# Four weight slots with the low part written in place, four bank pairs in the input loops: a two-layer diffusion trunk on one Trainium2 core

## The chip, the cores and the metric

The kernel runs on one core of a Trainium2 chip. The metric is the device time of one execution in microseconds (us), the median of several runs. A core has these engines: TensorE (PE in the profile) for matrix products, VectorE (DVE), ScalarE (ACT), GpSimd (POOL), and SyncE (SP), whose in-order queue issues nearly all DMA transfers here. Engines run side by side and order themselves by semaphores: an instruction waits until a semaphore has reached a number.

## The reference, cut to what matters

384 tokens (128 context, 256 latent) of width 1024 go through two layers. Each layer is a half-step FFN, a mixer, and a second half-step FFN; so there are four FFNs, which hold most of the arithmetic:

```python
def swiglu(h, w_in, w_out):                       # w_in 1024 x 5632, w_out 2816 x 1024
    gate, up = jnp.split(h @ w_in, 2, axis=-1)
    return (jax.nn.silu(gate) * up) @ w_out

def macaron_layer(x, mod, norm_g, ffn_in, ffn_out, mixer):
    m = mod[:, :, None, :]                        # mod = silu(cond) @ w_mod + b_mod
    x = x + 0.5 * m[:, 2] * swiglu(modulate(x, norm_g[0], m[:, 0], m[:, 1]), ffn_in[0], ffn_out[0])
    mixed, own_kv = mixer(modulate(x, norm_g[1], m[:, 3], m[:, 4]))
    x = x + m[:, 5] * mixed
    x = x + 0.5 * m[:, 8] * swiglu(modulate(x, norm_g[2], m[:, 6], m[:, 7]), ffn_in[1], ffn_out[1])
    return x, own_kv
```

Layer 0 mixes by attention beside a convolution, layer 1 by a Fourier mix beside a gated unit. Inputs are fp32, and `mod` is a product of two conditioning vectors with a 1024 x 9216 matrix in each layer.

## The kernel before

**Units.** All projection weights are cut into 153 units of 128 x 2048 fp32 values (1 MB) that are used in one fixed order: 33 for an FFN, 11 and 10 for the mixers. In an FFN the units 0 to 21 are input units (a gate tile and an up tile each) and 22 to 32 are output units. The text counts units from the start of an FFN. The code calls the four FFNs s = 0, 2, 3, 5; the text says first to fourth.

**The path of a unit.** SP loads it into a slot of `w_raw`; ACT copies it, rounded, to `w_hi` (`split` on ACT); DVE writes `w_lo = w_raw - w_hi` (`split` on DVE); PE runs 48 matmuls on it (`three`: hi*hi, hi*lo, lo*hi for each of 16 blocks). There are RING = 3 slots of each of the three tensors. The load of unit u waits until `w_lo` of unit u-3 is written (`lo_done`), since then the raw values are dead; ACT's `split` of u waits until PE is through with u-3 (`unit_done`), since then `w_hi` is free.

**Input loop.** `step` t of ACT and DVE first splits unit t+2; then ACT takes silu of the gate of unit t, DVE multiplies it by the up part, and both split the result into `h_hi` and `h_lo`. PE's unit t writes bank pair t % 3 of the PSUM, so it waits for the product of unit t-3 (`prod_done`).

**Output units** accumulate into all eight PSUM banks. The first one takes them in an order that starts with the banks that the last input units have left first.

**Modulation tiles.** `mod` for later stages is made on DVE beside the FFNs: a tile is a 128 x 1024 piece of `w_mod` (0.5 MB), multiplied by each of two conditioning rows with a sum along the row (`mod_tile`, two instructions). Three tile slots lie in the first halves of `m_raw`; the other halves hold the two rows and a scratch row for the first product. SP's load of tile n waits for tile n-3 (`tile_used`).

**Order on the queues.** SP, ACT and DVE execute in the order in which the code is written. SP's `load_ffn` and DVE's `ffn` mix units and tiles by hand-written tables: `TILES_BEFORE` tiles ahead of the loop, one tile in each loop step, then `TILES_OUT[s][j]` tiles in output iteration j, in which DVE splits unit 24+j and SP loads a unit and then that many tiles.

**End of an FFN.** Behind its last tiles DVE makes the gate, adds the eight 128-row blocks of the output to `x` (`residual`, which waits block by block for PE), and ACT and POOL sum the squares for the next norm. PE can only start the next stage when that norm is through.

Of the kernel before, what the change touches and what calls it, by code (L numbers as in the profile page):

```python
# [21 lines left out]
F32R = mybir.dt.float32r  # L22
# [4 lines left out]
P = 128  # L27
# [26 lines left out]
RING = 3  # L54
MRING = 3
UNIT = 2048
# [15 lines left out]
LOOPS = (FT - 1) // RING  # L72
FIRST_TILES = MRING * GROUPS_FIRST * PAIR_TILES
MOD_TILES = 2 * MODT - FIRST_TILES
TILES_BEFORE = {0: 3, 2: 0, 3: 0, 5: 2}
TILE_LOOPS = {0: LOOPS, 2: LOOPS, 3: LOOPS, 5: 2}
TILES_OUT = {0: [3, 3] + [2] * 8, 2: [2] + [1] * 9, 3: [3] + [2] * 8 + [0], 5: [0] * 10}
TILE0, _t = {}, 0
for _s in (0, 2, 3, 5):
    TILE0[_s] = _t  # L80
    _t += TILES_BEFORE[_s] + MRING * TILE_LOOPS[_s] + sum(TILES_OUT[_s])
assert _t == MOD_TILES and MRING == RING
# [87 lines left out]
def build(nc, x_prompt, x_sample, cache_k, cache_v, c, c_ctx, b_mod, norm_g,  # L170
# [4 lines left out]
    with ctx:  # L175
# [94 lines left out]
        tile_in = [sem(f"tile_in{i}") for i in range(MRING)]  # L270
# [61 lines left out]
        def mod_rows(b):  # L332
            return m_raw[:, b, 0:D_MODEL]

        def cond_row(cnd):
            return m_raw[:, cnd, D_MODEL:UNIT]

        def row_products():
            return m_raw[:, 2, D_MODEL:UNIT]
# [3 lines left out]
        def _(sp):  # L343
            def load_unit(u, i=0):

                sp.wait_ge(lo_done, u + 1 + RING * i)
                sp.dma_start(w_raw[:, slot(u), :].unsqueeze(1),
                             w_units[bass.ds(u + i * RING, 1)].rearrange("u p n -> p u n")).then_inc(raw_in[slot(u)], 16)
# [8 lines left out]
            def load_tile(n, i=0):  # L357

                if n >= MRING:
                    sp.wait_ge(tile_used, n - MRING + 1 + MRING * i)  # L360
                sp.dma_start(mod_rows(n % MRING).unsqueeze(1),
                             w_rows[bass.ds(n + MRING * i, 1)].rearrange("t p n -> p t n")).then_inc(tile_in[n % MRING], 16)

            def load_ffn(s):
# [137 lines left out]
        def _(act):  # L502
# [46 lines left out]
            def ffn(s):  # L549
# [12 lines left out]
                step(0, 0, 0)  # L562
                with act.Fori(0, LOOPS) as i:
                    for b in range(RING):
                        step(1 + b, (1 + b) % RING, i)
# [212 lines left out]
        def _(dve):  # L778
# [27 lines left out]
            def mod_tile(n, i=0):  # L806

                dve.wait_ge(tile_in[n % MRING], 16 * (n // MRING + 1) + 16 * i)
                if n:
                    dve.wait_ge(half_used, n + MRING * i)  # L810
                for cnd, out, done in ((0, row_products(), half_used), (1, mod_rows(n % MRING), tile_used)):
                    nc.vector.scalar_tensor_tensor(  # L812
                        out, mod_rows(n % MRING), 1.0, cond_row(cnd), ALU.mult, ALU.mult,
                        accum_out=mod_cols[:, bass.ds(FIRST_TILES + n + MRING * i, 1), cnd]).then_inc(done, 1)
# [73 lines left out]
            def ffn(s):  # L888
# [20 lines left out]
                step(0, 0, 0, None)  # L909
                done = 0  # L910
                for rounds, with_tiles in ((TILE_LOOPS[s], True), (LOOPS - TILE_LOOPS[s], False)):
                    if rounds:
                        with dve.Fori(0, rounds) as i:
                            for b in range(RING):
                                step(1 + RING * done + b, (1 + b) % RING, i, n + b if with_tiles else None)
                        done += rounds
                n += MRING * TILE_LOOPS[s]
# [262 lines left out]
        def _(pe):  # L1180
# [92 lines left out]
            def ffn(s):  # L1273
# [8 lines left out]
                with pe.Fori(0, LOOPS - 1) as i:  # L1282
                    for b in range(RING):
                        step(2 + b, i)
                for t in range(2 + RING * (LOOPS - 1), FT):
                    step(t, 0)
# [17 lines left out]
                with pe.Fori(0, (FFN_OUT_UNITS - 2) // RING) as i:  # L1304
                    for b in range(RING):
                        out_unit(u0 + FT + 1 + b, 1 + b, i)
                u = u0 + FFN_UNITS - 1
# [314 lines left out]
```

## Time and profile before

| what | value |
|---|---|
| median of 3 runs | 1500.81 us (1499.41 to 1501.71) |
| profiled execution | 1499.5 us, span in the profile 1497.7 us |
| PE busy | 1407.8 us, 94% of the span |
| DVE busy | 970.0 us, 65% |
| ACT busy | 557.7 us, 37% |
| DMA | 242.96 MB, mean 162 GB/s |

The profile is of one execution. Times of rows are in us from its start; "busy" counts an engine's own instructions, and a row's bracket says how long the engine was idle before it and what ended that. PE's share says that it is nearly always at work, so what counts is where it is not, and what would make it wait in new places.

### The profile page before, as it was taken

To read this page: it belongs to the slowest core of one execution; us is meant where nothing else is said; L and a number is where in the kernel's file an instruction comes from. 1 tells how busy PE (TensorE), PEld (TensorE's weight loads), DVE (VectorE), ACT (ScalarE), POOL (GpSimd) and SP (SyncE) were. 2 spreads that over 40 slices of the span, in tenths; PEclk is the share of its full clock that TensorE was granted. 3 is DMA by queue.
4 is the path that set the end of the run, shared out by engine and by line. 5 is a ranking of instruction groups with operands and counts; after the bars stand their busy time and mean duration, and the time that the engine had idled before them with its cause. 6 is when DMAs were issued, how large, how long until landed. Compare 5 with 4: busy or idle time off the path is not lost.

```text
span 1497.7 us, 21193 instructions
## 1 busy us (share of the span) xinstructions
PE 1407.8 (94%) x8134; PEld 1375.4 (92%) x8134; DVE 970.0 (65%) x1394; ACT 557.7 (37%) x731; POOL 122.5 (8%) x110
## 2 busy tenths in 40 slices
PE   5799999989866899999998999999989989999998
PEld 3799999989845799999998999999989989999998
DVE  2777678968998566666757666679763477444332
ACT  2433332237666443333224333332345343333221
POOL 1000000014555100000001000000021010000000
PEclk9899999989878999999998999999989999999999
DMA  8765655752200235555652555547523325433421
GB/s 325 261 231 176 203 177 200 285 182 96 86 32 29 102 133 201 188 191 174 234 181 85 197 193 185 193 149 295 219 99 134 126 85 186 137 122 130 141 84 42
DMA packets 45114, 242.96 MB, mean 162 GB/s; under 512 B 4997, under 2 KB 6889, under 8 KB 24328
## 3 DMA queue, kind: packets, MB, share of 16 engines
q1 hardware_dynamic: 44464, 241.99, 46.7%
q8 instruction: 32, 0.52, 0.1%
q10 hardware_dynamic: 600, 0.30, 0.1%
q14 instruction: 18, 0.15, 0.0%
HBM read 240.57 MB, written 1.70 MB: 162 GB/s over the span
## 4 chain that ended last, share of the span: by engine, by line
PE 83%; DVE 10%; DMA 2%; ACT 2%; issue 1%; POOL 1%; ACTq 0%; SPq 0%; DVEq 0%; POOLq 0%
PE ps L1185 27%; PE ps L1186 27%; PE ps L1187 27%; DVE conv L974 4%; DVE w_lo L790 1%; DMA conv_rows<-in_conv_w 1%; DVE n_full L876 1%; PE ps L1254 1%; DVE m_raw L812 1%; DVE smax L1039 1%; ACT w_hi L528 1%; DVE a_lo L883 0%; POOL n_acc L453 0%; DMA m_raw<-in_w_pairs 0%; PE ps L1554 0%
## 5 line engine op out<-in xcount | busy, mean ns | idle before, releaser
L1185 PE MATMUL ps<-a_hi,w_hi 128*128 128x384 f32 x1744 | 591.7, 339 | 19.1 <-DVE a_lo L883 14.0
L1186 PE MATMUL ps<-a_lo,w_hi 128*128 128x384 f32 x1744 | 588.5, 337 | 0.0
L1187 PE MATMUL ps<-a_hi,w_lo 128*128 128x384 f32 x1744 | 588.1, 337 | 0.0
L790 DVE TENSOR_TENSOR w_lo<-w_raw,w_hi 128x2048 fp32r<-128x2048 f32 x153 | 352.9, 2306 | 162.3 <-ACT w_hi L528 162.0
L528 ACT ACTIVATE w_hi<-w_raw 128x2048 fp32r<-128x2048 f32 x153 | 292.1, 1909 | 264.7 <-PE ps L1187 200.2
L1185 PEld LDWEIGHTS ps<-a_hi,w_hi 128*128 128x128 f32 x1744 | 332.1, 190 | 23.4 <-issue 10.0
L1186 PEld LDWEIGHTS ps<-a_lo,w_hi 128*128 128x128 f32 x1744 | 332.1, 190 | 0.1
L1187 PEld LDWEIGHTS ps<-a_hi,w_lo 128*128 128x128 f32 x1744 | 331.7, 190 | 0.0
L812 DVE SCALAR_TENSOR_TENSOR m_raw<-m_raw 128x1024 f32<-128x1024 f32 x252 | 296.0, 1220 | 1.0 <-ACT m_raw L589 1.0
L1187 PE MATMUL ps<-h_hi,w_lo 128*128 (+1 forms) x704 | 236.6, 336 | 0.0
L1186 PE MATMUL ps<-h_lo,w_hi 128*128 (+1 forms) x704 | 236.6, 336 | 0.0
L1185 PE MATMUL ps<-h_hi,w_hi 128*128 (+1 forms) x704 | 236.6, 336 | 0.0
L557 ACT ACTIVATE glu<-ps 128x384 f32<-128x384 f32 x88 | 43.4, 493 | 376.6 <-PE ps L1187 376.6
L895 DVE TENSOR_TENSOR glu<-glu,ps 128x384 f32<-128x384 f32 x88 | 48.7, 554 | 167.2 <-ACT glu L557 167.2
L1187 PEld LDWEIGHTS ps<-h_hi,w_lo 128*128 128x128 f32 x704 | 132.4, 188 | 0.0
L1185 PEld LDWEIGHTS ps<-h_hi,w_hi 128*128 128x128 f32 x704 | 132.4, 188 | 0.0
L1186 PEld LDWEIGHTS ps<-h_lo,w_hi 128*128 128x128 f32 x704 | 132.4, 188 | 0.0
L898 DVE TENSOR_TENSOR h_lo<-glu,h_hi 128x384 f32 (+1 forms) x88 | 49.2, 559 | 71.6 <-ACT h_hi L559 71.6
L453 POOL TENSOR_TENSOR n_acc<-n_sq 128x384 f32<-128x384 f32 x6 | 6.1, 1014 | 973.4 <-ACT n_sq L538 879.5
L559 ACT ACTIVATE h_hi<-glu 128x384 f32 (+1 forms) x88 | 46.2, 525 | 86.4 <-DVE glu L895 86.4
L473 POOL TENSOR_TENSOR conv<-conv,taps_buf 128x399 f32<-128x399 f32 x60 | 72.9, 1215 | 51.5 <-ACT taps_buf L618 45.6
L974 DVE SCALAR_TENSOR_TENSOR conv<-padded,conv_wt,conv 128x399 f32<-128x399 f32 x60 | 61.1, 1018 | 1.6
(179 smaller groups left out, 666.2 us busy)
## 6 DMA issues: line engine op xcount, KB each, us to landing
w_raw<-in_w_units SPq DMA_DIRECT2D x153, 1024.0 KB, 5.0
m_raw<-in_w_rows SPq DMA_DIRECT2D x126, 512.0 KB, 3.6
m_raw<-in_w_pairs SPq DMA_DIRECT2D x9, 1024.0 KB, 7.7
out<-x_nat SPq DMA_DIRECT2D x3, 512.0 KB, 3.1
x_nat<-in_x_sample SPq DMA_DIRECT2D x1, 1024.0 KB, 12.5
fourier<-in_k_fourier SPq DMA_DIRECT2D x1, 768.0 KB, 4.4
x_nat<-in_x_prompt SPq DMA_DIRECT2D x1, 512.0 KB, 10.7
m_raw<-in_c_ctx SPq DMA_DIRECT2D x1, 512.0 KB, 5.7
```

The source lines that it names most:

```text
L473: nc.gpsimd.tensor_tensor(acc, acc, taps_buf[:, n % TAP_BUFS, :], ALU.add).then_inc(tap_added, 1)
L528: nc.scalar.activation(w_hi[:, slot(u), :], w_raw[:, slot(u), :], ACT.Copy).then_inc(hi_done, 1)
L557: nc.scalar.activation(glu[:, 0, :], ps[:, 2 * b, 0:TOK], ACT.Silu).then_inc(silu_done, 1)
L559: nc.scalar.activation(h_hi[:, bass.ds(t + RING * i, 1), :], glu[:], ACT.Copy).then_inc(h_hi_done, 1)
L790: nc.vector.tensor_tensor(w_lo[:, slot(u), :], w_raw[:, slot(u), :], w_hi[:, slot(u), :].bitcast(FP32), ALU.subtract).then_inc(lo_done, 1)
L812: nc.vector.scalar_tensor_tensor(out, mod_rows(n % MRING), 1.0, cond_row(cnd), ALU.mult, ALU.mult, accum_out=mod_cols[:, bass.ds(FIRST_TIL ...
L895: nc.vector.tensor_tensor(glu[:, 0, :], glu[:, 0, :], ps[:, 2 * b + 1, 0:TOK], ALU.mult).then_inc(prod_done, 1)
L898: nc.vector.tensor_tensor(h_lo[:, bass.ds(t + RING * i, 1), :], glu[:], h_hi[:, bass.ds(t + RING * i, 1), :].bitcast(FP32), ALU.subtract). ...
L974: ins = nc.vector.scalar_tensor_tensor(conv[:, j, :], padded[:, j, k:k + CONV_N], conv_wt[:, j, k:k + 1], conv[:, j, :], ALU.mult, ALU.add)
L1185: mm(out, whi, mhi, start=start, stop=False)
L1186: mm(out, whi, mlo, start=False, stop=False)
L1187: return mm(out, wlo, mhi, start=False, stop=stop)
```

## The change

Both rings get a fourth place. `RING` becomes 4; `w_lo` shares its memory with `w_raw`, so that DVE writes the low part over the raw values. A raw slot is then free only when PE is through with the unit, and SP's load of unit u waits for `unit_done` of u-4. The tile ring becomes 4 (`TRING`): four tile slots fill `m_raw` slots 0 and 1, the two conditioning rows fill slot 2, and the scratch row is a new tensor `m_prod`. PE's input unit t uses bank pair t % 4. The loops have five rounds of four steps instead of seven of three, and the tables are written anew; each FFN keeps its number of tiles (46, 32, 40, 8).

```diff
-RING = 3
+RING = 4
 MRING = 3
+TRING = 4
@@
-LOOPS = (FT - 1) // RING
+LOOPS = (FT - 2) // RING
@@
-TILES_BEFORE = {0: 3, 2: 0, 3: 0, 5: 2}
+TILES_BEFORE = {0: TRING, 2: 0, 3: 0, 5: 0}
 TILE_LOOPS = {0: LOOPS, 2: LOOPS, 3: LOOPS, 5: 2}
-TILES_OUT = {0: [3, 3] + [2] * 8, 2: [2] + [1] * 9, 3: [3] + [2] * 8 + [0], 5: [0] * 10}
+TILES_OUT = {0: [3] * 2 + [2] * 8, 2: [2, 2] + [1] * 8, 3: [2] * 10, 5: [0] * 10}
@@
-        w_raw = sb("w_raw", [P, RING, UNIT])
+        r = ExitStack()
+        w_raw = sb("w_raw", [P, RING, UNIT], stack=r)
+        r.close()
+        w_lo = sb("w_lo", [P, RING, UNIT], F32R)
         w_hi = sb("w_hi", [P, RING, UNIT], F32R)
-        w_lo = sb("w_lo", [P, RING, UNIT], F32R)
         m_raw = sb("m_raw", [P, MRING, UNIT])
+        m_prod = sb("m_prod", [P, D_MODEL])
@@
             def load_unit(u, i=0):
 
-                sp.wait_ge(lo_done, u + 1 + RING * i)
+                sp.wait_ge(unit_done, u + 1 + RING * i)
@@
             def load_tile(n, i=0):
 
-                if n >= MRING:
-                    sp.wait_ge(tile_used, n - MRING + 1 + MRING * i)
+                if n >= TRING:
+                    sp.wait_ge(tile_used, n - TRING + 1 + TRING * i)
@@
-                n += MRING * TILE_LOOPS[s]
+                n += TRING * TILE_LOOPS[s]
                 for j, tiles in enumerate(TILES_OUT[s]):
-                    if j < FFN_OUT_UNITS - 2:
-                        load_unit(u0 + FT + 2 + j)
+                    load_unit(u0 + FT + 1 + j)
                     for _ in range(tiles):
                         load_tile(n)
                         n += 1
@@
                 step(0, 0, 0, None)
+                step(1, 1, 0, None)
@@
-                        for d in (2, 3, 4, 5, 6, 7, 0, 1) if first else range(KT):
-                            if first and h == 0 and d in (2, 4, 0):
-                                pe.wait_ge(prod_done, RING + FT * f + FT - {2: 2, 4: 1, 0: 0}[d])
+                        for d in (4, 5, 6, 7, 0, 1, 2, 3) if first else range(KT):
+                            if first and h == 0 and d % 2 == 0:
+                                pe.wait_ge(prod_done, RING + FT * f + FT - {4: 3, 6: 2, 0: 1, 2: 0}[d])
```

**DVE at the start of the first FFN.** The rows are DVE's instructions from the subtraction for unit 1 to the first step; two rows that read `m_raw` are one tile, and L790 is the subtraction for unit 2. Before:

```order
L790 TENSOR_TENSOR w_lo<-w_raw,w_hi 128x2048 [waits hi_done]
L812 SCALAR_TENSOR_TENSOR m_raw,mod_cols<-m_raw 128x1024 [waits tile_in0,silu_rows]
L812 SCALAR_TENSOR_TENSOR m_raw,mod_cols<-m_raw 128x1024
...
L812 SCALAR_TENSOR_TENSOR m_raw,mod_cols<-m_raw 128x1024 [waits half_used,tile_in2]
L812 SCALAR_TENSOR_TENSOR m_raw,mod_cols<-m_raw 128x1024
L790 TENSOR_TENSOR w_lo<-w_raw,w_hi 128x2048 [waits hi_done]
L895 TENSOR_TENSOR glu<-glu,ps 128x384 [waits silu_done]
```

And now:

```order
L791 TENSOR_TENSOR w_lo<-w_raw,w_hi 128x2048 [waits hi_done]
L813 SCALAR_TENSOR_TENSOR m_prod,mod_cols<-m_raw 128x1024 [waits tile_in0,silu_rows]
L813 SCALAR_TENSOR_TENSOR m_raw,mod_cols<-m_raw 128x1024
...
L813 SCALAR_TENSOR_TENSOR m_prod,mod_cols<-m_raw 128x1024 [waits half_used,tile_in3]
L813 SCALAR_TENSOR_TENSOR m_raw,mod_cols<-m_raw 128x1024
L791 TENSOR_TENSOR w_lo<-w_raw,w_hi 128x2048 [waits hi_done]
L896 TENSOR_TENSOR glu<-glu,ps 128x384 [waits silu_done]
```

Four tiles instead of three stand ahead of the subtraction for unit 2.

**SP behind the input loop of the first FFN.** `m_raw<-in_w_rows` is a tile's load, `w_raw<-in_w_units` a unit's. Before, the first row loads unit 24, and each unit stands ahead of the tiles of its own iteration:

```order
L347 DMA w_raw<-in_w_units 128x2048 [waits lo_done]
L361 DMA m_raw<-in_w_rows 128x1024 [waits tile_used] x3
L347 DMA w_raw<-in_w_units 128x2048 [waits lo_done]
L361 DMA m_raw<-in_w_rows 128x1024 [waits tile_used] x3
L347 DMA w_raw<-in_w_units 128x2048 [waits lo_done]
L361 DMA m_raw<-in_w_rows 128x1024 [waits tile_used] x2
```

Now the rows have the same form, but the first one loads unit 23:

```order
L348 DMA w_raw<-in_w_units 128x2048 [waits unit_done]
L362 DMA m_raw<-in_w_rows 128x1024 [waits tile_used] x3
L348 DMA w_raw<-in_w_units 128x2048 [waits unit_done]
L362 DMA m_raw<-in_w_rows 128x1024 [waits tile_used] x3
L348 DMA w_raw<-in_w_units 128x2048 [waits unit_done]
L362 DMA m_raw<-in_w_rows 128x1024 [waits tile_used] x2
```

So unit 24, which was loaded ahead of the tiles of iteration 0, now stands behind them, and unit 24+j behind those of iteration j; a tile's load waits for the tile four before it, not three, and a unit's for PE instead of DVE.

## Rows read from the trace of the kernel before

**Rows 1.** The page, part 1: busy time, share of the span, instructions.

```profile
PE 1407.8 (94%) x8134; PEld 1375.4 (92%) x8134; DVE 970.0 (65%) x1394; ACT 557.7 (37%) x731; POOL 122.5 (8%) x110
```

**Rows 2.** Waits of PE: in total, how often, the longest (us).

```profile
PE ps L1185 <- DVE a_lo L883: 14.0, 6, 2.9
...
PE ps L1185 <- DVE w_lo L790: 3.3, 2, 1.7
```

**Rows 3.** Timeline of PE: the first matmuls of units 2, 3 and 26.

```profile
67.53 0.45 PE L1185 MATMUL ps<-a_hi,w_hi 128*128 128x384 f32 x1 [1.60 <-DVE w_lo L790]
...
75.97 0.33 PE L1185 MATMUL ps<-a_hi,w_hi 128*128 128x384 f32 x1
...
267.32 0.34 PE L1185 MATMUL ps<-h_hi,w_hi 128*128 x1
```

**Rows 4.** Timeline of DVE: third tile, then the subtraction for unit 2.

```profile
62.90 1.22 DVE L812 SCALAR_TENSOR_TENSOR m_raw<-m_raw 128x1024 f32<-128x1024 f32 x1
...
64.05 1.22 DVE L812 SCALAR_TENSOR_TENSOR m_raw<-m_raw 128x1024 f32<-128x1024 f32 x1
...
65.19 2.29 DVE L790 TENSOR_TENSOR w_lo<-w_raw,w_hi 128x2048 fp32r<-128x2048 f32 x1
```

**Rows 5.** Timeline of SP's queue behind the input loop of the first FFN.

```profile
239.00 0.33 SPq L361 DMA_DIRECT2D m_raw<-in_w_rows  x1
239.37 0.43 SPq L347 DMA_DIRECT2D w_raw<-in_w_units  x1
243.49 4.91 SPq L361 DMA_DIRECT2D m_raw<-in_w_rows  x3
248.45 0.43 SPq L347 DMA_DIRECT2D w_raw<-in_w_units  x1
...
255.79 0.43 SPq L347 DMA_DIRECT2D w_raw<-in_w_units  x1
```

**Rows 6.** Timeline of ACT there: the copies for units 25 and 26.

```profile
246.56 1.92 ACT L528 ACTIVATE w_hi<-w_raw 128x2048 fp32r<-128x2048 f32 x1 [8.78 <-DMA w_raw<-in_w_units]
255.97 1.92 ACT L528 ACTIVATE w_hi<-w_raw 128x2048 fp32r<-128x2048 f32 x1 [7.49 <-DMA w_raw<-in_w_units]
```

**Rows 7.** Timeline of DVE there: subtractions for units 22, 23, 24.

```profile
222.36 2.29 DVE L790 TENSOR_TENSOR w_lo<-w_raw,w_hi 128x2048 fp32r<-128x2048 f32 x1
...
230.65 2.29 DVE L790 TENSOR_TENSOR w_lo<-w_raw,w_hi 128x2048 fp32r<-128x2048 f32 x1
...
238.89 2.29 DVE L790 TENSOR_TENSOR w_lo<-w_raw,w_hi 128x2048 fp32r<-128x2048 f32 x1
```

**Rows 8.** DMA issues of 90 to 220, 236 to 264, 1020 to 1056 us: median landing.

```profile
w_raw<-in_w_units SPq DMA_DIRECT2D x16, 1024.0 KB, 5.1
...
w_raw<-in_w_units SPq DMA_DIRECT2D x4, 1024.0 KB, 7.5
...
w_raw<-in_w_units SPq DMA_DIRECT2D x5, 1024.0 KB, 5.8
```

**Rows 9.** Loads of units from 200 to 330 us, all.

```profile
DMA to landing us min/median/max: 4.9/6.2/9.8
```

**Rows 10.** Timelines around the end of the first FFN: DVE, PE.

```profile
315.57 2.29 DVE L790 TENSOR_TENSOR w_lo<-w_raw,w_hi 128x2048 fp32r<-128x2048 f32 x1 [5.95 <-ACT w_hi L528]
...
322.78 5.29 DVE L852 SCALAR_TENSOR_TENSOR x<-ps,m_gate,x 128x128 f32<-128x128 f32 x16
...
325.39 0.34 PE L1187 MATMUL ps<-h_hi,w_lo 128*128 128x384 f32 x1
...
339.03 0.69 PE L1185 MATMUL ps<-a_hi,w_hi 128*128 128x384 f32 x1 [2.14 <-DVE a_lo L883]
```

**Rows 11.** The same places at the end of the third FFN.

```profile
1081.20 0.74 DVE L852 SCALAR_TENSOR_TENSOR x<-ps,m_gate,x 128x128 f32<-128x128 f32 x2 [4.91 <-PE ps L1187]
...
1088.03 0.34 PE L1187 MATMUL ps<-h_hi,w_lo 128*128 128x384 f32 x1
...
1097.72 0.66 PE L1185 MATMUL ps<-a_hi,w_hi 128*128 128x384 f32 x1 [2.23 <-DVE a_lo L883]
```

More of the change, by code:

```diff
@@ L80 @@
     TILE0[_s] = _t
-    _t += TILES_BEFORE[_s] + MRING * TILE_LOOPS[_s] + sum(TILES_OUT[_s])
-assert _t == MOD_TILES and MRING == RING
+    _t += TILES_BEFORE[_s] + TRING * TILE_LOOPS[_s] + sum(TILES_OUT[_s])
+assert _t == MOD_TILES and TRING == RING
 LAYER_PAIRS = MODT // PAIR_TILES
@@ L269, in build @@
         mod_used = sem("mod_used")
-        tile_in = [sem(f"tile_in{i}") for i in range(MRING)]
+        tile_in = [sem(f"tile_in{i}") for i in range(TRING)]
         half_used, tile_used = sem("half_used"), sem("tile_used")
@@ L332, in mod_rows @@
         def mod_rows(b):
-            return m_raw[:, b, 0:D_MODEL]
+            return m_raw[:, b // 2, b % 2 * D_MODEL:(b % 2 + 1) * D_MODEL]
         def cond_row(cnd):
-            return m_raw[:, cnd, D_MODEL:UNIT]
-        def row_products():
-            return m_raw[:, 2, D_MODEL:UNIT]
+            return mod_rows(TRING + cnd)
         @block.sync
@@ L562, in ffn @@
                 step(0, 0, 0)
+                step(1, 1, 0)
                 with act.Fori(0, LOOPS) as i:
                     for b in range(RING):
-                        step(1 + b, (1 + b) % RING, i)
+                        step(2 + b, (2 + b) % RING, i)
                 split(u0 + FT + 2)
@@ L806, in mod_tile @@
             def mod_tile(n, i=0):
-                dve.wait_ge(tile_in[n % MRING], 16 * (n // MRING + 1) + 16 * i)
+                dve.wait_ge(tile_in[n % TRING], 16 * (n // TRING + 1) + 16 * i)
                 if n:
-                    dve.wait_ge(half_used, n + MRING * i)
-                for cnd, out, done in ((0, row_products(), half_used), (1, mod_rows(n % MRING), tile_used)):
+                    dve.wait_ge(half_used, n + TRING * i)
+                for cnd, out, done in ((0, m_prod[:], half_used), (1, mod_rows(n % TRING), tile_used)):
                     nc.vector.scalar_tensor_tensor(
-                        out, mod_rows(n % MRING), 1.0, cond_row(cnd), ALU.mult, ALU.mult,
-                        accum_out=mod_cols[:, bass.ds(FIRST_TILES + n + MRING * i, 1), cnd]).then_inc(done, 1)
+                        out, mod_rows(n % TRING), 1.0, cond_row(cnd), ALU.mult, ALU.mult,
+                        accum_out=mod_cols[:, bass.ds(FIRST_TILES + n + TRING * i, 1), cnd]).then_inc(done, 1)
             def mod_ready(tiles):
@@ L914, in ffn @@
                             for b in range(RING):
-                                step(1 + RING * done + b, (1 + b) % RING, i, n + b if with_tiles else None)
+                                step(2 + RING * done + b, (2 + b) % RING, i, n + b if with_tiles else None)
                         done += rounds
-                n += MRING * TILE_LOOPS[s]
+                n += TRING * TILE_LOOPS[s]
                 for j, tiles in enumerate(TILES_OUT[s]):
@@ L1281, in ffn @@
                 first_units(u0, (0, 2), s, s != 0)
-                with pe.Fori(0, LOOPS - 1) as i:
+                with pe.Fori(0, LOOPS) as i:
                     for b in range(RING):
                         step(2 + b, i)
-                for t in range(2 + RING * (LOOPS - 1), FT):
-                    step(t, 0)
                 def out_unit(u, t, i, first=False):
@@ L1303, in ffn @@
                 pe.wait_ge(h_ready, 1 + FT * (f + 1))
-                with pe.Fori(0, (FFN_OUT_UNITS - 2) // RING) as i:
+                rounds = (FFN_OUT_UNITS - 2) // RING
+                with pe.Fori(0, rounds) as i:
                     for b in range(RING):
                         out_unit(u0 + FT + 1 + b, 1 + b, i)
+                for t in range(1 + RING * rounds, FFN_OUT_UNITS - 1):
+                    out_unit(u0 + FT + t, t, 0)
                 u = u0 + FFN_UNITS - 1
```

4 lines of the change are left out of this document (2 added, 2 removed).

## The prediction, made before the changed kernel was run

> **What bounds the kernel now.** I read the page's busy times first: PE works 94% of the span [rows 1]. Then PE's waits. The only ones inside an FFN's run of units are two for `w_lo`, 3.3 us together [rows 2]; the rest sits where a norm or a mixer stands between two runs. The timeline of PE shows the second of the two: unit 2 starts at 67.53 after a wait, unit 3 at 75.97, unit 26 at 267.32 [rows 3]. That is 191.35 us for 23 units, 8.32 us each, so from unit 3 on PE never paused. This says at once what the fourth bank pair can bring: a product that PE waits for doesn't occur in PE's list, so it removes nothing. The same holds for a deeper ring in the steady part. A gain can only lie where PE stands still now, and a loss wherever the new order makes a unit late by more than its lead.
>
> **Start of the first FFN.** DVE runs the tiles ahead of the subtraction for unit 2, and PE waits for exactly that subtraction: it starts at 65.19, directly behind the third tile, and PE starts at 67.53, directly behind it [rows 3, 4]. A tile takes 65.19 - 62.90 = 2.29 us [rows 4]. The fourth tile stands in the same place, with nothing to cover it: **+2.3 us**. DVE's backlog is not passed on further: everything behind moves by the same 2.3 us, PE too. The tile that is saved in step 1 comes after the subtraction that matters. In what follows I use the times of the old trace, without these 2.3 us.
>
> **Input loops.** A unit's load now waits until PE is through with the unit four before. ACT wants unit t+2 only behind the work for unit t-1; the load starts when unit t-2 ends, one unit (8.32 us) earlier, and such loads land in 5.1 us [rows 8]. So some 3 us and the silu work for unit t-1 cover it, and behind that PE's own lead of a unit; if that cover went, ACT would be late by the difference, and PE would see it only beyond some 5 us more. The mixers I cost at nothing for the same reason: their loads are issued when the fourth unit before ends, and ACT's copy stands behind the second or third.
>
> **Output units of the first FFN.** Here the order on SP's queue decides. Iteration j held: load unit 24+j, then its tiles. Now unit 24+j stands behind the tiles of iteration j, and a tile's load waits for the tile four before, which DVE must have finished. So a unit's load waits for DVE, and DVE's next subtraction waits for that load: a loop through four parts. I work it out by these pieces:
>
> - from the end of a tile on DVE to the issue of the unit's load behind it: the tile's own issue first, then 0.37 us [rows 5], together 0.45 us;
> - landing L;
> - ACT's copy 1.92 us, DVE's subtraction 2.2 us, with the handovers 4.25 us. The old rows agree: issued at 248.45, copy begun at 255.97 [rows 5, 6].
>
> For L there are rows of both kinds: four loads around 250 us landed in 7.5 (median), five at 1020 to 1056 us in 5.8 [rows 8]; in both places each followed a tile's load closely. I take 7.1 for unit 25 and 7.4 for unit 26, which go out where the old loads were slow, and 5.8 after them.
>
> Now in order. The tile of step 20 ends at 230.65, where the subtraction for unit 23 starts [rows 7]; unit 24's load goes at 231.1 and is there before DVE wants it at 238.9 [rows 7]. The three tiles of iteration 0 end at 243.5, 245.8, 248.1. The third tile of iteration 1 waits for the second of these, and unit 25 behind it is issued at 246.2; it went at 239.37 [rows 5]. Its low part is ready at 246.2 + 7.1 + 4.25 = 257.6; PE wants it at 267.32 - 8.32 = 259.0. Then comes the first tile of iteration 1, until 259.9, which releases unit 26's load at 260.3 (it went at 248.45 [rows 5]). Ready at 260.3 + 7.4 + 4.25 = 272.0, wanted at 267.3: **PE stands for 4.7 us**.
>
> From there every second unit closes the loop: two tiles (4.6), 0.45, L, 4.25, in sum 15.1 us at L = 5.8, against 16.64 us that PE takes for two units. So PE waits no more, but DVE gains only 1.5 us on PE in two units. Low parts of units 28, 30, 32 are ready at 287.1, 302.2, 317.3; the two tiles behind the last, the subtraction for unit 33 (2.2), two more tiles (4.6) and the gate (0.4) put the residual at 329.1. It started at 322.78 [rows 10]. PE, 4.7 us later than before, is through with its last unit at about 330, so the residual, 5.3 us long, is behind PE there too, and the norm behind it moves with it: **+6.3 us**. The stall of PE is inside this sum and isn't added to it.
>
> The old boundary was late already: from the last matmul to the first of the next stage 13.6 us (325.39, 339.03), where the third FFN needs 9.7 (1088.03, 1097.72) since its DVE waited 4.9 us for PE before the residual [rows 10, 11]. That 3.9 us is all that this place could give back.
>
> **The other FFNs.** The second has one tile in most iterations, so DVE's share of the loop halves and the loads are soon released by PE alone: nothing. The third now has two tiles in every iteration, the last one included. By the same recurrence, with L = 5.8 to 6.5, its gate is ready before PE delivers the first block: nothing; at 7.4 it is 4 us late. The fourth has no tiles in its output part.
>
> **Sum.** 2.3 + 6.3 = 8.6 us. The profiled execution took 1499.5 us, 1.3 below the median; on the median this gives 1500.8 + 8.6 = **1509.4 us**. A measurement tells 0.2% (3 us) from no change.
>
> **What L does.** L = 5.75 throughout gives the residual at 325.9 (+3.1, sum 5.4, 1506.2 us). L = 7.4 throughout gives a loop of 16.7 us, as long as PE's, the residual at 334.2 (+11.4), and with the third FFN's 4 us a sum of 17.7: 1518.5 us. The page "DMA: Bandwidth & Descriptors" of the Trainium skill, in its section on the anatomy of one DMA, prices a transfer at about 2.0 us plus its bytes over 436 GB/s (it fits another issuing path); by it a unit alone would take an estimated 4.4 us and a unit with the tile ahead of it 5.6. With 4.4 the sum would be near -1.5 us, with 5.6 near +4.6. The old trace doesn't agree with the lower of these: its fastest load in this stretch took 4.9, the median was 6.2 [rows 9].
>
> **Rivals.**
>
> *The loop keeps up (not slower).* One mechanism: loads land fast enough that unit 26 isn't late and DVE catches up. With L = 4.8 unit 26 is ready at 267.0, the loop takes 14.1 us, and the residual comes at 321.2, 1.6 us earlier than now. With the start's 2.3 us that is 1501.5 us. It turns into a gain only below L = 4.7. For it: single loads of 4.9 us [rows 9], and less traffic from one side, since loads are spaced further apart. Against it: every one of these loads has a tile's load right ahead of it, and such ones took 5.8 or more in the median [rows 8]. The Trainium skill ("Trainium Kernel Development and Optimization", Best Practices) advises double buffering so that DMA and compute overlap; read simply, a fourth place should help. Its gain would have to come from the 3.9 us above.
>
> *Every load is slow.* L near 7.4 throughout and the third FFN late too: 1514 to 1518.5 us. For it: the four loads around 250 us [rows 8]. Against: those overlapped the unit before, which the new spacing avoids.
>
> *Only the start costs.* If I have the queue's waits wrong and units are still ahead, the sum is 2.3 us: 1503 us. Against it stand the rows of SP above: the tiles' loads came out at DVE's pace even with the old order [rows 5].
>
> *The mixers.* If a raw load there came late, ACT would hold back the taps for POOL, 1 to 3 us. PE's list has no wait for `w_lo` there that it would lengthen [rows 2]; I leave it in the range.
>
> **How the numbers follow.** Forecast (5 to 12 us slower, PE late at unit 26 and a late residual): 0.60. Loop slow throughout or the third FFN late as well, above 1513: 0.16. Only the start or a loop that nearly keeps up, 1500 to 1504: 0.16. A gain of over 3 us, for which landing would have to be under 4.7 and the start hidden: 0.05; a loss from a place that I cost at nothing (the mixers, an input loop): 0.03. Range: 1502 to 1517 us; the forecast's own is 1505 to 1513. Slower by over 0.2%: 0.79, within 0.2%: 0.16, faster: 0.05.
>
> **What would show it.** PE's wait for `w_lo` before unit 2 grows from 1.6 to 3.9 us. A new wait of PE for `w_lo`, 2 to 6 us, stands before unit 26, the fifth output unit of the first FFN. SP issues unit 25 some 7 us later against PE than now and unit 26 some 12. DVE's subtractions there wait for ACT, and ACT for `w_raw`'s DMA, every second unit. From the last matmul of the first FFN to the next stage it is 13.6 us plus 1 to 3 instead of 9.7. The three other FFNs keep units of 8.32 us and their boundaries. I am wrong if unit 26 isn't late, if the boundary falls to 10 us, or if waits turn up in the input loops or the mixers.

## The result and the profile after

| | before | after |
|---|---|---|
| median of 5 runs each, side by side | 1501.71 us (1499.41 to 1503.12) | 1514.75 us (1512.49 to 1519.90) |
| profiled execution, span | 1499.5, 1497.7 us | 1515.96, 1514.2 us |
| mean granted clock | 0.964 | 0.959 |

The changed kernel is slower: the ratio is 1.0091, 95% interval 1.0076 to 1.0107. On the medians that is 13.0 us, between the two profiled executions 16.5 us. This difference and all but one of those below are under 2%; where an interval leaves out 1, I call the kernel slower or faster.

Busy times of the page, then PE's waits for `w_lo`, as in [rows 1, 2]:

```profile
PE 1417.0 (94%) x8134; PEld 1383.7 (91%) x8134; DVE 969.4 (64%) x1394; ACT 559.3 (37%) x731; POOL 120.2 (8%) x110
```

```profile
PE ps L1187 <- DVE w_lo L791: 9.4, 4, 3.9
```

The work is the same, and yet PE is busy 9.2 us longer. Waits for `w_lo` are 9.4 us instead of 3.3. The first number can't be a wait: the same 8134 matmuls took longer. 2.7 us of it are in unit 2, as shown next, and 5.1 us in the first mixer (see "Left open" below). The timeline of PE shows the places, as in [rows 3, 10]: units 2, 3, 26, then the last matmul of the first FFN and the first of the mixer.

```profile
69.23 0.69 PE L1187 MATMUL ps<-a_hi,w_hi 128*128 128x384 f32 x1 [3.86 <-DVE w_lo L791]
...
74.84 0.52 PE L1189 MATMUL ps<-a_hi,w_lo 128*128 128x384 f32 x1
...
75.38 0.33 PE L1188 MATMUL ps<-a_lo,w_hi 128*128 128x384 f32 x1
...
80.41 0.33 PE L1187 MATMUL ps<-a_hi,w_hi 128*128 128x384 f32 x1
...
275.01 0.44 PE L1187 MATMUL ps<-h_hi,w_hi 128*128 x1 [3.08 <-DVE w_lo L791]
...
334.22 0.34 PE L1189 MATMUL ps<-h_hi,w_lo 128*128 128x384 f32 x1
...
352.71 0.69 PE L1187 MATMUL ps<-a_hi,w_hi 128*128 128x384 f32 x1 [2.14 <-DVE a_lo L884]
```

Unit 2 waits 3.86 us instead of 1.60, and then its matmuls stand 0.32 us apart until 75 us, and 0.17 us after that. It takes 11.18 us, not 8.44. The windows say the same of the clock (columns: window, its length, busy us of PE, PEld, DVE, ACT and POOL with their instructions, granted clock, DMA share, GB/s). After:

```profile
70.00:80.00 10.00, 10.00 (x45) 10.00 (x45) 6.16 (x5) 4.71 (x5) 0.00 (x0) 0.74 0.11 43
```

And before:

```profile
70.00:80.00 10.00, 10.00 (x60) 10.00 (x59) 8.28 (x9) 3.94 (x6) 0.00 (x0) 1.00 0.80 285
```

PE is busy in all ten microseconds of both, but has 45 matmuls there where it had 60; the mean granted clock is 0.74, so it was at the lower level (1.2 of 2.4 GHz) for about the first half.

Output units of the first FFN: SP's queue [rows 5], ACT's copies for units 25 and 26 [rows 6], and DVE's subtractions for them:

```profile
250.60 0.43 SPq L348 DMA_DIRECT2D w_raw<-in_w_units  x1
252.52 12.27 SPq L362 DMA_DIRECT2D m_raw<-in_w_rows  x2
264.83 0.43 SPq L348 DMA_DIRECT2D w_raw<-in_w_units  x1
```

```profile
257.90 1.92 ACT L528 ACTIVATE w_hi<-w_raw 128x2048 fp32r<-128x2048 f32 x1 [14.84 <-DMA w_raw<-in_w_units]
270.62 1.91 ACT L528 ACTIVATE w_hi<-w_raw 128x2048 fp32r<-128x2048 f32 x1 [10.80 <-DMA w_raw<-in_w_units]
```

```profile
259.84 2.29 DVE L791 TENSOR_TENSOR w_lo<-w_raw,w_hi 128x2048 fp32r<-128x2048 f32 x1 [7.35 <-ACT w_hi L528]
...
272.56 2.29 DVE L791 TENSOR_TENSOR w_lo<-w_raw,w_hi 128x2048 fp32r<-128x2048 f32 x1 [3.56 <-ACT w_hi L528]
...
329.29 2.29 DVE L791 TENSOR_TENSOR w_lo<-w_raw,w_hi 128x2048 fp32r<-128x2048 f32 x1 [1.68 <-ACT w_hi L528]
...
336.49 5.29 DVE L853 SCALAR_TENSOR_TENSOR x<-ps,m_gate,x 128x128 f32<-128x128 f32 x16
```

Every link of the loop is there: the queue stands 12 us at a tile's load, the unit's load goes when DVE has ended a tile, ACT waits for that load, DVE for ACT, PE for DVE. Since unit 3 began 4.44 us later than before, a time of the old trace is one of these less 4.44. The residual comes at 332.05 by the old clock instead of 322.78 [rows 10], and it never waits for PE.

From here "start to start of unit u" is the time from the first matmul of unit u-1 to that of unit u, over the whole program (33 is the mixer's first unit, 44, 77 and 110 are the first of the next three stages, 120 that of the last FFN). In us, from the timelines of PE; the names are those of the experiments below:

| unit | before | after | e1 | e2 | e3 | e4 | e6 | e12 | e8 | e10 |
|---|---|---|---|---|---|---|---|---|---|---|
| 2 | 10.19 | 12.48 | 10.20 | 12.49 | 10.20 | 10.20 | 10.19 | 10.20 | 10.19 | 10.20 |
| 3 | 8.44 | 11.18 | 8.43 | 11.11 | 8.45 | 8.46 | 8.43 | 8.43 | 8.44 | 8.44 |
| 26 | 8.32 | 11.57 | 10.98 | 8.32 | 8.33 | 8.32 | 8.32 | 8.32 | 8.32 | 8.32 |
| 27 | 8.32 | 8.42 | 10.00 | 8.32 | 8.32 | 8.32 | 8.32 | 8.32 | 8.32 | 8.32 |
| 28 | 8.32 | 9.27 | 8.32 | 8.32 | 8.32 | 8.32 | 8.32 | 8.32 | 8.32 | 8.32 |
| 33 | 21.79 | 26.64 | 24.95 | 16.93 | 16.93 | 17.74 | 26.83 | 25.71 | 16.92 | 16.92 |
| 44 | 17.70 | 17.02 | 17.01 | 17.02 | 17.01 | 17.70 | 23.66 | 19.06 | 17.01 | 16.92 |
| 77 | 17.83 | 17.02 | 17.01 | 17.02 | 17.02 | 17.84 | 24.02 | 19.06 | 16.91 | 17.01 |
| 110 | 17.84 | 17.88 | 21.03 | 17.03 | 16.85 | 17.69 | 23.72 | 19.06 | 17.02 | 17.02 |
| 120 | 17.01 | 16.97 | 16.80 | 17.02 | 17.02 | 17.02 | 22.16 | 19.06 | 17.01 | 16.83 |

The first FFN accounts for 2.29 (wait before unit 2) + 2.74 (its low clock) + 3.25 + 0.10 + 0.95 (units 26 to 28) + 4.85 (boundary) = 14.2 us of the loss between the two profiled executions. The first mixer adds 3.4 us, the boundaries at 44 and 77 give 1.5 back.

### The profile page after: what moved, and what is told of

Same layout as the page of the kernel before. It is cut to its first block, busy times and chain, and to the rows that moved or that the text cites. A ratio compares the mean times of both kernels' runs of the same rounds, so it can differ in the third digit from the quotient of the medians.

```text
span 1514.2 us, 21053 instructions
## 1 busy us (share of the span) xinstructions
PE 1417.0 (94%) x8134; PEld 1383.7 (91%) x8134; DVE 969.4 (64%) x1394; ACT 559.3 (37%) x731; POOL 120.2 (8%) x110
## 4 chain that ended last, share of the span: by engine, by line
PE 78%; DVE 12%; DMA 4%; ACT 2%; issue 2%; POOL 1%; ACTq 0%; SPq 0%; DVEq 0%; POOLq 0%
PE ps L1187 25%; PE ps L1188 25%; PE ps L1189 25%; DVE conv L976 4%; DMA w_raw<-in_w_units 2%; DVE w_lo L791 2%; DVE m_prod L813 1%; DMA conv_rows<-in_conv_w 1%; ACT w_hi L528 1%; DVE n_full L877 1%; PE ps L1256 1%; DVE m_raw L813 1%; DVE smax L1041 1%; DVE a_lo L884 0%; POOL n_acc L453 0%
## 5 line engine op out<-in xcount | busy, mean ns | idle before, releaser
L813 DVE SCALAR_TENSOR_TENSOR m_prod<-m_raw 128x1024 f32<-128x1024 f32 x126 | 153.6, 1219 | 1.0 <-ACT m_raw L590 1.0
L813 DVE SCALAR_TENSOR_TENSOR m_raw<-m_raw 128x1024 f32<-128x1024 f32 x126 | 153.8, 1220 | 0.0
```

Source lines behind the costliest of these rows:

```text
L813: nc.vector.scalar_tensor_tensor(out, mod_rows(n % TRING), 1.0, cond_row(cnd), ALU.mult, ALU.mult, accum_out=mod_cols[:, bass.ds(FIRST_TIL ...
```

## The experiments

Each ran in five rounds beside the kernel before, whose medians in the three sets were 1502.36, 1502.40 and 1501.96 us.

**The fourth tile behind step 1** (e1), on DVE alone:

```diff
-                for _ in range(TILES_BEFORE[s]):
+                late = 1 if s == 0 else 0
+                for _ in range(TILES_BEFORE[s] - late):
                     mod_tile(n)
                     n += 1
                 step(0, 0, 0, None)
                 step(1, 1, 0, None)
+                for _ in range(late):
+                    mod_tile(n)
+                    n += 1
```

> The changed kernel, with DVE's fourth tile of the first FFN moved from ahead of step 0 to behind step 1; nothing else. Theory (the start costs a tile plus the low clock that the longer wait brings): unit 2 of PE waits 1.6 us as in the kernel before instead of 3.9 and runs at 8.4 us instead of 11.2; 2.3 + 2.7 = 5 us less than the changed kernel, about 1510 us against 1502 of before; the output part of the first FFN keeps its loss of about 9 us. Rival (the slow unit 2 has another cause, such as DMA traffic of the earlier loads beside it): unit 2 stays at 11 us, and only 2.3 us come back.

Measured 1509.72 us (1508.13 to 1513.20), ratio 1.0053 (1.0039 to 1.0068): 5.0 us under the changed kernel. Units 2 and 3 are back at 10.20 and 8.43 us. One tile of 2.3 us cost 5.0, as the wait that it made longer cost the clock too (e7 below shows that). The output part of the first FFN lost 7.5 us here (units 26, 27 and 33 of the table), not 9. The profiled execution of e1, the slowest of its six, was late by 3.2 us at unit 110, the end of the third FFN, where DVE's residual ran through without a wait for PE, which had been 4.91 us [rows 11]:

```profile
1094.62 5.29 DVE L853 SCALAR_TENSOR_TENSOR x<-ps,m_gate,x 128x128 f32<-128x128 f32 x16
```

**A unit's load ahead of its tiles again** (e2), SP alone:

```diff
-                    load_unit(u0 + FT + 1 + j)
+                    if j == 0:
+                        load_unit(u0 + FT + 1)
+                    if j < FFN_OUT_UNITS - 2:
+                        load_unit(u0 + FT + 2 + j)
```

> The changed kernel, with SP's order behind the input loops as before: unit 24+j ahead of the tiles of iteration j (unit 33 still behind them). Theory (the loss of the output part is the loop SP - DMA - ACT - DVE that this order closed): the waits of PE before units 26 and 28 vanish, the subtractions for units 25 to 33 no longer wait for late loads, the residual of the first FFN waits for PE, and the way from the last matmul to the next stage falls from 16.2 us to the 9.7 of the third FFN: 13 us less than the changed kernel, about 1502 us, level with before. Rival (the tile ring of four or the loads' wait for PE is the cause, not the place in the queue): the stall at unit 26 stays and the time falls by under 3 us.

Measured 1499.93 us (1497.63 to 1502.04), ratio 0.9985 (0.9976 to 0.9993). That is 14.8 us under the changed kernel, where 13 were expected. Units 26 to 28 are at 8.32 us and the boundary at 16.93, which is 4.9 better than before, though the order is that of before. The timelines of DVE and of SP show where that comes from:

```profile
318.87 0.17 DVE L848 TENSOR_TENSOR m_gate<-mod_cols,vec_a 128x16 f32<-128x16 f32 x1
...
323.07 0.74 DVE L856 SCALAR_TENSOR_TENSOR x<-ps,m_gate,x 128x128 f32<-128x128 f32 x2 [3.82 <-PE ps L1192]
```

```profile
297.35 5.39 SPq L362 DMA_DIRECT2D m_raw<-in_w_rows  x4
305.30 25.29 SPq L348 DMA_DIRECT2D w_raw<-in_w_units  x4
```

DVE now waits 3.8 us for PE ahead of the residual, which it had started at once [rows 10]. The first of the four loads of units is issued at 305.30, 300.8 by the old clock (unit 3 began 4.5 us later than before here), against 307.73 in the kernel before. I read it so that with four tile slots the last tiles' loads wait for earlier tiles and the queue gets past them sooner; that alone wasn't tried.

**Both repairs, and the load of unit 33 ahead of the last tiles** (e3): e1's and e2's edits and the lines below, which hold for the first three FFNs. The load is taken out of its old place at the start of the next stage (not shown).

```diff
-                    if j < FFN_OUT_UNITS - 2:
+                    if j < FFN_OUT_UNITS - 2 or s < 5:
```

> Both repairs together: fourth tile behind step 1, units ahead of the tiles, and unit 33 too ahead of the last tiles. Theory: nothing of the loss stays, and the first FFN's boundary is down to 9.7 us, so 3.5 to 4 us less than the kernel before: about 1498 us. Rival (the four slots or the write in place cost something by themselves, such as in the mixers): at or above 1502 us.

Measured 1494.86 us (1493.77 to 1497.04), ratio 0.9956 (0.9943 to 0.9969): faster than both kernels, and 3 us under the 1498 expected.

**That load alone, in the kernel before** (e4):

> The kernel before (three slots), with only the load of unit 33 moved ahead of the last iteration's tiles. Theory (the late boundary of the first FFN came from this load): it goes at 305 us instead of 307.7, the residual starts about 2.7 us earlier, and the time falls by 2 to 3 us to 1499: most of what the four slots bring after repair would be had without them. Rival (a deeper ring is needed for it): no change, 1502 us.

Measured 1498.68 us (1495.84 to 1499.69), ratio 0.9975 (0.9967 to 0.9984). The edit moves the same load in the first three FFNs, but only the boundary at 33 changes much: it falls by 4.1 us, those at 77 and 110 by 0.2 at most. So the 3.9 us read from [rows 10, 11] were there to be had. Between e4 and e3 lie 3.8 us that neither theory had: the table shows 0.7 to 0.8 us at each of units 33, 44, 77 and 110. The timelines around unit 77, of POOL, DVE and ACT, first of the kernel before:

```profile
799.02 4.47 POOL L453 TENSOR_TENSOR n_acc<-n_acc,n_sq 128x384 f32<-128x384 f32 x4
```

```profile
802.45 0.17 DVE L835 TENSOR_TENSOR m_shift<-mod_cols,vec_b 128x16 f32<-128x16 f32 x1
802.53 0.99 DVE L836 TENSOR_TENSOR m_scale<-mod_cols,vec_b 128x16 f32<-128x16 f32 x1
```

```profile
793.53 1.92 ACT L528 ACTIVATE w_hi<-w_raw 128x2048 fp32r<-128x2048 f32 x1 [6.46 <-PE ps L1187]
795.46 1.28 ACT L532 ACT_TABLE_LOAD   x1
```

Then of e3:

```profile
794.35 4.47 POOL L457 TENSOR_TENSOR n_acc<-n_acc,n_sq 128x384 f32<-128x384 f32 x4
```

```profile
798.71 0.17 DVE L840 TENSOR_TENSOR m_shift<-mod_cols,vec_b 128x16 f32<-128x16 f32 x1
798.79 0.17 DVE L841 TENSOR_TENSOR m_scale<-mod_cols,vec_b 128x16 f32<-128x16 f32 x1
```

```profile
786.26 1.92 ACT L532 ACTIVATE w_hi<-w_raw 128x2048 fp32r<-128x2048 f32 x1 [6.46 <-DMA w_raw<-in_w_units]
```

Two instructions of the same shape take 0.17 and 0.99 us, and the long one ends at 803.52, 0.03 us behind POOL's last add at 803.49. In e3 the add ends at 798.82, and the same instruction, from 798.79 on, takes 0.17. The rows suggest that DVE is held until POOL's add is over if it starts early in the add, and that POOL is late in the old kernel because ACT's table load stands behind a copy that waits for PE; with a fourth slot that copy waits for a load instead. It fits that the first of the two instructions, at 802.45, wasn't held: POOL was idle from 802.35 to 802.49, between two of its adds, and the held one started 0.04 us into the next. The page "SBUF — State Buffer" of the Trainium skill, section "Who interferes with whom", states that a VectorE instruction with two SBUF inputs contends with a GpSimd instruction that reads SBUF. The trace agrees, with 0.8 us. But in e3 the instruction at 798.71 started in the last 0.11 us of an add and took 0.17 all the same.

**The table load moved, in three-slot kernels** (e8 on top of e4, e11 on the kernel before alone):

```diff
                 if s < 5:
+                    preload(s + 1, ACT.Sqrt)
                     split(u0 + FFN_UNITS + 1)
```

The same goes ahead of the copy at the end of the first mixer, and `norm_stats` leaves it out there.

> The kernel before with the load of unit 33 of each FFN issued ahead of the last tiles (as in e4_before_unit33_early, 1498.68 us), and ACT's load of the square-root table moved ahead of its copy of the next stage's second unit at the ends of the stages. Theory (at the boundaries of a three-slot kernel DVE's tiny scale of the running sum of squares takes 0.86 to 1.00 us, and not 0.17, since it is held until GpSimd's add on the same sums is over, and that add is late because ACT's table load stands behind a copy that waits for PE): GpSimd's adds come about 0.9 us earlier, the scale takes 0.17 us at the boundaries, three or four boundaries are shorter by 0.8 us each, and the time is 1495.5 to 1497 us. Rival (the boundary is set by other work, or the holding moves along with the adds): 1498 to 1499 us, scales of 0.86 us and more still there.

> The kernel before with the early square-root table load alone, the order of its loads unchanged. Theory: GpSimd's adds come earlier and DVE's scale takes 0.17 us at the four later boundaries of the kernel; three of them (1 to 2, 2 to 3, 3 to 4) are shorter by 0.7 to 0.8 us, and the first is still late by its own loads: 1499 to 1500.5 us, against 1502.4 for the kernel before. Rival (the gain of e8_before_early_preload over e4_before_unit33_early was chance): within 0.1% of the kernel before, 1501 to 1504 us.

e8: 1494.38 us (1493.23 to 1496.65), ratio 0.9952 (0.9938 to 0.9966), 4.3 us under e4 (2 to 3 expected). e11: 1499.59 us (1497.59 to 1501.93), ratio 0.9981 (0.9972 to 0.9990), 2.4 us under the kernel before. Around unit 77 of e8, POOL and DVE:

```profile
793.62 4.48 POOL L454 TENSOR_TENSOR n_acc<-n_acc,n_sq 128x384 f32<-128x384 f32 x4
```

```profile
798.07 0.17 DVE L840 TENSOR_TENSOR m_scale<-mod_cols,vec_b 128x16 f32<-128x16 f32 x1
```

What the hold costs can be told apart from what POOL's late adds cost. PE's sum over POOL's result and DVE's next subtraction, behind which the norm goes on, of the kernel before and then of e8:

```profile
803.83 0.81 PE L1247 MATMUL ps<-ones,n_acc 128*128 128x1 f32 x6
803.76 2.29 DVE L790 TENSOR_TENSOR w_lo<-w_raw,w_hi 128x2048 fp32r<-128x2048 f32 x1
```

```profile
799.37 0.81 PE L1251 MATMUL ps<-ones,n_acc 128*128 128x1 f32 x6
798.49 2.29 DVE L794 TENSOR_TENSOR w_lo<-w_raw,w_hi 128x2048 fp32r<-128x2048 f32 x1
```

The last matmul of the FFN starts at 801.41 and 796.95. PE's sum comes 2.42 us behind it in both, so the late adds as such delay nothing; DVE's subtraction comes 2.35 us behind it and 1.54, the 0.8 us of the held instruction.

All scales at the stage ends of e8 take 0.17 or 0.18 us. In e11 those at 44, 77 and 110 do; the one at 33, where the residual is late anyway, took 1.01. So both runs bear out the reading of the rows: the boundaries at 44, 77 and 110 are shorter by 2.5 us together in e11, which gained 2.4, and the four of e8 by 3.1 us of its 4.3 over e4. The rest of e8's gain I can't place.

**Both repairs with the table load moved** (e10):

> The version with both repairs (e3_both_repaired, 1494.86 us) with the early square-root table load of e8_before_early_preload as well. Theory (the early table load and the fourth slot give back the same 0.8 us at four boundaries, since either lets GpSimd's adds come earlier, so their gains don't add): 1494 to 1496 us. Rival (they are separate gains of 3 to 4 us): 1490.5 to 1492 us.

Measured 1494.92 us (1493.63 to 1496.73), ratio 0.9953 (0.9941 to 0.9965). It is e3 again, so the two gains are one. Three slots with two edits of order (e8) do as well as four slots, written in place, with everything repaired: the fourth slot bought nothing that order didn't.

**Three bank pairs in the changed kernel** (e5). The pair of the fourth step is that of the second, and PE waits for the product of the unit two before:

```diff
-                    pe.wait_ge(prod_done, FT * f + t + 1 + RING * i)
-                    in_unit(u0 + t, 2 * (t % RING), i)
+                    pe.wait_ge(prod_done, FT * f + t + 3 + RING * i)
+                    in_unit(u0 + t, 2 * (1 if t % RING == 3 else t % RING), i)
```

> The changed kernel with three bank pairs again in the input loops: the fourth step of each round uses the second pair once more, and PE waits for the product of two (not three) units before, as deep as it can. All else stays, four weight slots and tables too. Theory (the fourth pair brings nothing, since PE never waits for a product in the input loops): within 1 us of the changed kernel, 1513 to 1516 us, no PE wait for a product of DVE. Rival (DVE's products now come late enough behind four-step rounds that the pair is needed): PE waits at each fourth unit of an input loop, 20 places, and the time is over 1517 us.

Measured 1517.70 us (1517.09 to 1521.86), ratio 1.0112 (1.0093 to 1.0131), whose interval overlaps that of the changed kernel. The timeline of PE has four waits for a product, this one and three of 0.21 us:

```profile
71.71 0.68 PE L1187 MATMUL ps<-a_hi,w_hi 128*128 128x384 f32 x1 [4.42 <-DVE glu L896]
```

All four stand before the third unit of an FFN (units 2, 46, 79 and 122 of the program). That unit uses the third pair, which neither of the two units before it has; the edit makes every unit wait for the product of the unit two before, also where its pair is free. So these waits come from the way the edit is written, in all 4.42 - 3.86 + 3 x 0.21 = 1.2 us, and are no price of the missing pair. Before the units that share the second pair, PE has no wait for a product of 0.15 us or more. The theory's reason holds, though its number was missed: the median lies 1.7 us above its range, inside the rival's, whose 20 waits are not there. Nothing in these runs shows that the fourth pair is worth anything.

**In place with three slots** (e6): the kernel before, with `w_lo` over `w_raw` and

```diff
-                sp.wait_ge(lo_done, u + 1 + RING * i)
+                sp.wait_ge(unit_done, u + 1 + RING * i)
```

> The kernel before with three slots and its old order and tables, but with the low part written over the raw weights, so that a unit's load waits for PE to be through with the unit three before (in place without a fourth slot). Theory (in the mixers and input loops the load then starts one unit's time before ACT wants it, 8.3 us against a landing of 5 to 6 us plus the work in front, and no slack for ACT's copy of unit t+2): ACT waits for the raw unit's DMA in most steps of the input loops, copy and subtraction end only some 0 to 1 us ahead of PE, and the time is 3 to 8 us above the kernel before: 1505 to 1510 us. This would be what the fourth slot pays for. Rival (the lead is still enough everywhere): within 0.2% of the kernel before, 1499 to 1505 us. A second rival: PE waits for w_lo in every input unit by 1 us or more, 80 units, over 1560 us.

Measured 1540.29 us (1538.85 to 1541.60), ratio 1.0253 (1.0239 to 1.0268): 38 us, outside all three ranges. ACT does wait for 129 of the 153 loads, as I had said, and in the input loops this costs nothing: their units keep 8.32 us. The loss lies where I hadn't looked, 5 to 6 us at each of five boundaries, and 9 us in the two mixers (against the profile before, whose first mixer was the shortest of all). The timeline of ACT ahead of unit 44:

```profile
524.87 1.92 ACT L530 ACTIVATE w_hi<-w_raw 128x2048 fp32r<-128x2048 f32 x1 [10.86 <-DMA w_raw<-in_w_units]
526.80 1.28 ACT L534 ACT_TABLE_LOAD   x1
...
528.21 3.40 ACT L540 ACTIVATE n_sq<-x 128x384 f32<-128x384 f32 x8
```

The norm's eight squares stand behind the copy of the next stage's second unit, whose load waits for PE. They run in one piece of 3.4 us when it is through, since their input had been waiting.

**The same with that copy behind the squares** (e12):

```diff
                     nc.scalar.activation(n_sq[:, d, :], x[:, d, :], ACT.Square).then_inc(sq_done, 1)
+                if unit is not None:
+                    split(unit)
@@
-                if s < 5:
-                    split(u0 + FFN_UNITS + 1)
```

The mixers' ends are changed in the same way (not shown).

> The low part in place with three slots (e6_in_place_three_slots, 1540.29 us), with ACT's copy of the next stage's second unit moved behind its eight squares at the ends of the five later norms' stages. Theory (the 5 to 6 us that each of five boundaries lost there came from ACT's squares standing behind that copy, whose load waits for PE to be through with the second last unit of the stage; with a fourth slot the load can go one unit earlier): each boundary gives 3.5 to 5 us back, less 1.4 us for the copy and subtraction now in front of DVE's share of the norm: the time falls by 12 to 22 us, to 1518 to 1528 us. Rival (the boundaries are late since the first units of the next stage come late themselves): 1538 to 1541 us.

Measured 1520.87 us (1519.90 to 1523.58), ratio 1.0132 (1.0116 to 1.0147): 19.4 us come back. Ahead of unit 44 the copy is now last:

```profile
528.92 0.52 ACT L540 ACTIVATE n_sq<-x 128x384 f32<-128x384 f32 x1 [1.56 <-DVE x L852]
529.35 1.89 ACT L530 ACTIVATE w_hi<-w_raw 128x2048 fp32r<-128x2048 f32 x1
```

Four boundaries are at 19.06 us, 2.0 above those with a fourth slot. The two mixers stay as long as in e6. So in place three slots were 18.9 us slower than the kernel before even in this order, and with four slots and both repairs (e3) nothing of that is left: the fourth slot pays back what writing in place takes away. Three slots in place with every edit of order together weren't tried.

**Work in PE's wait** (e7): 20 matmuls, which the computation has no use for, between units 1 and 2 of the first FFN of the changed kernel:

```diff
                 first_units(u0, (0, 2), s, s != 0)
+                if s == 0:
+                    for _ in range(20):
+                        mm(ps[:, 6, 0:TOK], a_hi[:, 0, 0:P], a_hi[:, 0, :], start=True, stop=True)
```

> The changed kernel with 20 more matmuls (128x128 by 384 columns, of operands that are there anyway, into a bank that is free) on PE between units 1 and 2 of the first FFN, 3.5 us of work inside its wait of 3.9 us; their result is not used. Theory (unit 2 took 11.2 us and not 8.4 since PE's granted clock fell to the lower of its levels behind the longer wait): with the wait filled, unit 2 takes 8.4 us again, its first matmul not 0.69 us each, and the time falls by 2.5 to 2.8 us to about 1512 us. Rival (unit 2 is slow for another reason, such as operands that come late or DVE's and ACT's work beside it): unit 2 stays at 11.2 us and the time at 1514.7 us. If the filler itself runs at the lower clock, it takes 6.9 us and the time is 3 us longer than that of the changed kernel.

Measured 1512.12 us (1510.48 to 1516.98), ratio 1.0075 (1.0058 to 1.0092), 2.6 us under the changed kernel for more work done. The intervals of the two ratios overlap, so the profile has to show it. The timeline of PE, and the window to set beside the two above:

```profile
65.74 3.63 PE L1286 MATMUL ps<-a_hi 128*128 128x384 f32 x20
69.78 0.44 PE L1187 MATMUL ps<-a_hi,w_hi 128*128 128x384 f32 x1 [0.41 <-DVE w_lo L791]
```

```profile
70.00:80.00 10.00, 10.00 (x59) 10.00 (x59) 6.32 (x7) 5.53 (x6) 0.00 (x0) 1.00 0.25 76
```

Unit 2 starts as late as in the changed kernel (12.49 us after unit 1) and takes 8.45 us, not 11.18. DVE is busy as long as there (6.32 and 6.16 us of the ten) and the DMA share is 0.25 against 0.11, both far under the 0.80 of the kernel before, so it was PE's own standing still that cost the clock.

## Why the prediction was right, and where it fell short

**The direction and both places were right.** PE's wait before unit 2 grew from 1.6 to 3.9 us as said; PE stood before unit 26; the residual was late; the second FFN and all input loops kept 8.32 us. e1 and e2 take each part away alone; e2 gets its part back in full, e1 its 5.0 us. 1514.75 us lies in the range, but above the forecast's own 1505 to 1513, where I had put other mechanisms: the loop slow throughout, or the third FFN late. Neither is what the profiled execution shows. The sum of 8.6 us left out 2.7 us of clock and 2.9 us of landings and of the wait for unit 33's load, and 1.5 us that came back; with them it is 12.7, next to the 13.0 of the medians. The profiled executions differ by 3.4 us more, in the first mixer. That the number stayed inside 1502 to 1517 is owed in part to the width of the range.

**Start of the first FFN: +2.3 said, +5.0 measured.** The step "everything behind moves by the same 2.3 us" failed: PE ran unit 2 in part at the lower clock, 2.7 us. e7 shows the cause. [Rows 3] held the hint, a first matmul of 0.45 us behind 1.60 us of waiting, and 0.69 behind the longer waits of [rows 10]; I read the waits and not the durations behind them. The page "TensorE: Matmul & The Clock Gate" of the Trainium skill, section "HAM oscillation — how this bites in real kernels", describes a kernel that loses its clock at each DMA wait. The trace agrees for this wait, here for DVE, and says what it costs; behind the 3.08 us before unit 26 the granted clock stayed at 1.00.

**Output part of the first FFN: +6.3 said, +9.2 measured** (3.25 + 0.10 + 0.95 + 4.85). The recurrence holds, the landings were mis-sized, term by term on the old clock:

| step | predicted | measured |
|---|---|---|
| unit 25's load issued | 246.2 | 246.16 |
| unit 26's load issued | 260.3 | 260.39 |
| its landing | 7.4 | 5.7 |
| unit 26 ready | 272.0 | 270.33 |
| unit 28 ready (its load landed in 8.4) | 287.1 | 288.02 |
| units 30, 32 ready | 302.2, 317.3 | 303.1, 318.5 |
| unit 33 ready | 324.1 | 327.1 |
| residual | 329.1 | 332.05 |

The two issue times are right within 0.1 us. I took the slow landing at unit 26, where it was 5.7, and none behind it, where 8.4 came at unit 28; by unit 32 that is 1.2 us. My argument against slow landings, that they came from overlap with the unit before, doesn't hold either: unit 28's load went 3.2 us after the one before it had landed, and in the old trace the load issued at 248.45 took 7.4 us though the one before it was there at 246.45. The last step was wrong in kind: I took unit 33 as ready behind the two tiles, but its own load is in the same loop, landed in 7.5 us, and DVE waited 1.68 us for it. So the stretch from the last matmul to the next stage is 18.5 us (334.22, 352.71), where I had said 13.6 plus 1 to 3.

**Third FFN: nothing said.** In the profile of the changed kernel that is true (17.88 against 17.84), but the slack of 4.9 us [rows 11] is gone: DVE starts the residual at once and does ten of its sixteen instructions in one piece.

```profile
1098.80 3.34 DVE L853 SCALAR_TENSOR_TENSOR x<-ps,m_gate,x 128x128 f32<-128x128 f32 x10
```

In e1's it was late by 3.2 us. The prediction had "4 us late" at L = 7.4; this place is on the edge, and may be one source of the spread between executions, which only the profiled ones could show.

**Ring and bank pairs: nothing said, 1.5 us gained.** True of the loops. The boundaries at 44 and 77 give 0.7 and 0.8 us, since the copy ahead of the table load no longer waits for PE (e8, e10). That four slots cost nothing, though `w_lo` lies over `w_raw`, is right, and e6 shows how little I knew of the reason: I checked ACT's lead in the loops, and it is the boundary that decides.

**Left open.** The first mixer (from unit 33 to unit 43) took 167.9 us in the profile before and 171.3 after, 3.4 us of the 16.5. Its windows, before and after:

```profile
339.03:506.90 167.87, 136.05 (x787) 0.87 0.19 64
352.71:524.00 171.29, 141.15 (x787) 0.85 0.17 59
```

PE is busy 5.1 us longer with the same 787 matmuls (here the columns are busy us of PE, granted clock, DMA share, GB/s), so its matmuls ran slower, and it waited no longer than before. The stretch took 169.0 to 171.7 us in nine of the variants, three-slot ones among them, and 174.9 and 176.0 in e6 and e12. So I don't put the 3.4 us down to the change; what sets them wasn't tried.

## What to carry to other kernels

Where loads share an in-order queue, ask of each load what the instruction in front of it waits for; a load that a late consumer waits for belongs ahead of loads that wait for that consumer. At the end of a stage, work for the next one (a copy, a table load) must not stand ahead of what the boundary needs: with one load of a unit put earlier, that was worth as much here as a fourth buffer. Price a new PE wait with the work behind it, at either clock.

## What the runs showed of the hardware

- A wait of 3.86 us before unit 2 was followed by matmuls 0.32 us apart instead of 0.17 for about 6 us, 2.7 us in all. Behind waits of 1.6 us at the same place the unit took 8.44 us instead of 8.32, so 0.1 us more. Before unit 26, 3.08 us cost 0.1 us behind it, and 2.50 us in e1 cost 1.7 (unit 27 at 10.00 us; granted clock 0.83 from 270 to 280 us): the length of one wait alone doesn't say it.
- An instruction of DVE on 16 columns that started 0.04 us into an add of POOL took 0.99 us instead of 0.17, and ended 0.03 us behind the add. One that started in the last 0.11 us of an add took 0.17.
